# Hybrid encoder: heads in the order B, C, A, two maps scored at once, probabilities turned by half banks, out-projection begun beside the last pair

## The chip, the cores and the metric

The kernel runs on one core of a Trainium2 chip. The metric is the device time of one execution in microseconds (us), as the median of several runs.

## The reference, cut to what matters

Two layers of mixing and MLP over 1024 positions of width 1024, all in float32, then a last RMSNorm. The mixing has 4 differential heads (A, two softmax maps each, values 128 wide), 4 windowed heads with sinks (B, a window of two blocks of 128) and 4 forgetting heads (C, causal, with a cumulative gate).

```python
for l in range(DEPTH):                       # DEPTH = 2
    h = rmsnorm(x, g_mix[l])
    proj = h @ w_in[l]                       # q, k, v of A, B, C and the gates of C
    # A, per head, for each block of 128 queries against all keys up to its end:
    s = q @ k.T * scale - slope * |pos_q - pos_k|         # two maps m = 0, 1
    a = softmax(s[0]) - lam * softmax(s[1])
    o_a = rmsnorm(a @ v, a_subln[l]) * (1 - lam_init)
    # B: the same with one map, a window of 128 keys, and a sink in the softmax's sum
    # C: one map
    s = q @ k.T * scale + cum[q] - cum[k]    # cum = cumsum(log_sigmoid(cf + bias))
    o_c = softmax(where(pos_k <= pos_q, s, NEG)) @ v
    x = x + concat(o_a, o_b, o_c) @ w_out[l]
    h = rmsnorm(x, g_mlp[l])
    x = x + square(relu(h @ w_up[l])) @ w_down[l]         # 1024 -> 4096 -> 1024
return rmsnorm(x, g_final)
```

## The kernel before

Activations lie transposed: feature chunks of 128 on the partitions, 1024 positions along the free dimension. Every large product is done in a split form: an operand becomes a high part (rounded to the matmul's format, a copy on ScalarE) and a low part (the difference, on VectorE), and three products high x high, high x low, low x high are added in PSUM. A **slab** is one 128-column strip of a weight matrix times all positions. It has 8 **pieces** (one per chunk of 128 inputs, `piece`, line 1192, and `products`, 1136), each of 6 matmuls of 512 columns. A weight slab is loaded in two DMAs on SyncE's queue into the single buffer `w_raw` (`load`, 366) and split into one of two slots (ScalarE 477 and 525, VectorE 809 and 841). The next load waits for that split.

The kernel has five instruction streams written out by hand, one per engine, each in its own order, tied by counting semaphores. A wait in a stream holds all that stands behind it.

A layer goes so. The 23 input slabs give gates, then q, k and v for eight **pairs**: an A pair is one head with its two maps, a C pair two heads, a B pair two query heads that share keys. A slab's result is scaled out of PSUM into `part` (`evacuate`, 847), copied to the high part (527) and subtracted to the low part (843); values are turned first by eight transposes (`turn`, 1153). From the fifth slab on, the pieces stand as filling between the steps of attention, for the pair after the current one.

`Run` (105) plans attention: `RUN_A` (two A pairs, executed twice by a loop), then `RUN_C`, then `RUN_CB` (the second C pair and both B pairs). `PIECES` and `END_PIECES` (99, 100) give the pieces beside each step; the last B pair has none, the first 8. An A step is one block of 128 queries with both maps, a C step one head of a block (16 a pair), a B step both heads of a block. `attend` on TensorE (1303) does in step t: scores of t (`scores`, 1259: three matmuls of up to 512 columns for each 512 keys, with only 64 contracted rows, map 0 on partitions 0 to 63, map 1 on 64 to 127), pieces, values of step t-2 (1283), in A the second map's scores, the transposes of step t-1 (`turn_probs`, 1271), pieces. All maps of A and C go through the same PSUM tensor `ps[0]`, one after another; B's two maps take a bank each.

```python
for at in range(0, width, BANK):
    w = min(BANK, width - at)
    for p, (q, k) in enumerate(((q_hi, k_hi), (q_hi, k_lo), (q_lo, k_hi))):
        mm = nc.tensor.matmul(ps[0][:, p0 + at:p0 + at + w], q[half, qs, i * P:(i + 1) * P],
                              k[half, ks, k0 * P + at:k0 * P + at + w], start=(p == 0), stop=(p == 2))
```

VectorE adds the position bias and takes the row maximum of a map in one custom instruction over its whole width (`biased_max`, 933, instruction at 940), scales it (946, 948), combines A's two maps (`combine`, 952 to 961), takes the low half of the turned probabilities (922, at 925 for the first four blocks, 929 for the rest) and sums the value parts (979). ScalarE does the exponentials with their row sums (632), the high half of the turned probabilities (600, 604), the finished outputs (615 to 627), and for C a bias of the key's and the query's cumulative gate (594, with 1003 on VectorE). Its gate rows are spread over the partitions by matmuls (`spread`, 1214): heads 0 and 1 before attention, 2 and 3 between `RUN_C` and `RUN_CB`. In each step ScalarE has: turned probabilities, exponentials, outputs, weight split. A turned step of up to 1024 columns fills `ps[2]`, both banks, so the next one's transposes wait for its low part (`pt_split`).

After the last step the eight head outputs are turned and split (`turn_out`, 1391; 702, 1052), with the first out-projection slab's pieces between them (1408), then the other seven slabs, each added to `xt`. That region held the head outputs during attention, so x was spilled to DRAM in one 4 MB DMA on SyncE's queue ahead of the third slab's load (396) and comes back in two of 2 MB (406). Then the MLP: 64 slabs, `up` and `down`, with ScalarE and VectorE taking the next weights before the hidden values (`split_w` ahead of `hidden`, 731 and 1093).

## Time and profile before

| what | us |
|---|---|
| three runs, median (lowest to highest) | 2849.33 (2838.36 to 2854.39) |
| the profiled execution | 2837.89 |
| its span, first to last instruction | 2835.8 |
| granted clock of TensorE over the span | 0.965 of full |
| TensorE busy | 2723.2 |
| VectorE, ScalarE, GpSimd busy | 1226.4, 958.7, 92.5 |

The profile is of one execution of its own, 2837.89 us, which lies at the low end of the three runs. Busy times are sums over the span. Matmuls overlap in the pipeline, so the mean duration of one (389 ns for 512 columns) is longer than the distance from one to the next. "PE" is TensorE's matmuls, "PEld" its weight loads, "DVE" VectorE, "ACT" ScalarE, "POOL" GpSimd, "SP" SyncE, and L1149 is line 1149 of the kernel. PEclk is the share of full clock that was granted in a fortieth of the span.

### The profile page before, as it was taken

The page shows a single profiled execution, that of the slowest core. Times are in us where ns is not written, and L with a number is a line of the kernel's source. Part 1 is how long each engine was busy: PE and PEld are TensorE (multiplying, and loading weights), DVE is VectorE, ACT ScalarE, POOL GpSimd, SP SyncE. Part 2 cuts the span into 40 slices and gives each one's busy share as a digit, 9 for nine tenths or more (in the row PEclk, how much of TensorE's full clock was granted, in tenths as well). Part 3 has the DMA queues.
Part 4 walks back from the last instruction along what each step waited for, and adds up shares of the span by engine and source line. Part 5 has one row for each costly group of instructions (what it writes and reads, how often), then busy time and mean ns, then how long its engine had stood idle before and what let it go on. Part 6 is the DMA issues. An engine that isn't in the chain of part 4 may idle for free.

```text
span 2835.8 us, 35362 instructions
## 1 busy us (share of the span) xinstructions
PE 2723.2 (96%) x12809; PEld 2211.0 (78%) x12809; DVE 1226.4 (43%) x2444; ACT 958.7 (34%) x1700; POOL 92.5 (3%) x51
## 2 busy tenths in 40 slices
PE   7999999979999999999999999998899999999998
PEld 6777777768888888888877777776788888888887
DVE  5565665654322322223436666656443223232334
ACT  4444454552321212112234444545423122130223
POOL 0000010001000000000200001000020000000001
PEclk9999999959999999999999999998899999999998
DMA  4100000012111111111130000000211111111112
GB/s 153 38 23 23 22 23 16 8 38 82 45 52 45 47 50 49 47 50 46 44 104 23 23 22 23 16 23 8 82 52 45 45 51 48 48 44 52 44 52 74
DMA packets 214389, 126.25 MB, mean 45 GB/s; under 512 B 14702, under 2 KB 213400, under 8 KB 213528
## 3 DMA queue, kind: packets, MB, share of 16 engines
q1 hardware_dynamic: 211176, 121.95, 14.4%
q10 hardware_dynamic: 3120, 3.15, 0.3%
q8 instruction: 48, 0.79, 0.1%
q14 instruction: 45, 0.37, 0.0%
HBM read 112.49 MB, written 12.58 MB: 44 GB/s over the span
## 4 chain that ended last, share of the span: by engine, by line
PE 84%; DVE 6%; ACT 4%; issue 3%; DVEq 1%; DMA 1%; SPq 0%; ACTq 0%; POOL 0%; POOLq 0%
PE ps L1149 54%; PE ps L1196 17%; PE ps L1266 5%; PE ps L1296 2%; PE ps L1278 1%; ACT probs L632 1%; PE ps L1298 1%; DVE probs L940 1%; PE ps L1155 1%; DVEq L943 1%; DVE part L856 1%; PE ps L1408 1%; PE ps L1218 1%; DVE neg_max L948 1%; DVE part L853 1%
## 5 line engine op out<-in xcount | busy, mean ns | idle before, releaser
L1149 PE MATMUL ps<-h_hi,w_hi 128*128 128x512 f32 x1024 | 315.6, 389 | 0.0
L1060 DVE TENSOR_TENSOR xt<-ps,xt 128x1024 f32 (+1 forms) x80 | 98.0, 1225 | 503.1 <-PE ps L1149 501.6
L1149 PE MATMUL ps<-h_lo,w_hi 128*128 128x512 f32 x1024 | 315.3, 389 | 0.0
L1149 PE MATMUL ps<-u_hi,w_hi 128*128 128x512 f32 x1024 | 315.2, 389 | 0.0
L1149 PE MATMUL ps<-u_lo,w_hi 128*128 128x512 f32 x1024 | 315.2, 389 | 0.0
L1149 PE MATMUL ps<-h_hi,w_lo 128*128 128x512 f32 x1024 | 315.2, 389 | 0.0
L1149 PE MATMUL ps<-u_hi,w_lo 128*128 128x512 f32 x1024 | 315.2, 389 | 0.0
L477 ACT ACTIVATE w_hi<-w_raw 128x1024 fp32r<-128x1024 f32 x144 | 151.2, 1050 | 454.8 <-PE ps L1149 436.5
L1196 PE MATMUL ps<-h_hi,w_hi 128*128 128x512 f32 x736 | 265.5, 443 | 34.4 <-DVE v_parts L845 12.7
L1196 PE MATMUL ps<-h_lo,w_hi 128*128 128x512 f32 x736 | 237.4, 405 | 0.0
L1196 PE MATMUL ps<-h_hi,w_lo 128*128 128x512 f32 x736 | 235.0, 401 | 0.0
L720 ACT ACTIVATE ring<-ring 128x1024 f32<-128x1024 f32 x64 | 67.8, 1060 | 487.1 <-DVE ring L1080 487.1
L1149 PEld LDWEIGHTS ps<-h_lo,w_hi 128*128 128x128 f32 x1024 | 192.2, 188 | 40.0
L1149 PEld LDWEIGHTS ps<-h_hi,w_lo 128*128 128x128 f32 x1024 | 192.2, 188 | 40.0
L1149 PEld LDWEIGHTS ps<-u_lo,w_hi 128*128 128x128 f32 x1024 | 192.2, 188 | 39.9
L1149 PEld LDWEIGHTS ps<-u_hi,w_hi 128*128 128x128 f32 x1024 | 192.2, 188 | 39.9
L1149 PEld LDWEIGHTS ps<-u_hi,w_lo 128*128 128x128 f32 x1024 | 192.2, 188 | 39.9
L1149 PEld LDWEIGHTS ps<-h_hi,w_hi 128*128 128x128 f32 x1024 | 191.9, 188 | 39.6
L1080 DVE SCALAR_TENSOR_TENSOR ring<-ps,inv_rms 128x1024 f32<-128x1024 f32 x64 | 78.4, 1225 | 322.9 <-PE ps L1149 311.0
L1296 PE MATMUL ps<-v_parts,pt_hi 128*128 128x128 f32 (+1 forms) x696 | 182.0, 327 | 24.6 <-DVE pt_lo L929 18.6
L632 ACT ACTIVATE probs<-probs,neg_max,slope_now 128x256 f32<-128x256 f32 (+7 forms) x128 | 111.2, 868 | 255.7 <-DVE neg_max L946 255.5
L1196 PEld LDWEIGHTS ps<-h_hi,w_hi 128*128 128x128 f32 x736 | 120.9, 195 | 87.4 <-issue 57.3
(159 smaller groups left out, 4000.3 us busy)
## 6 DMA issues: line engine op xcount, KB each, us to landing
w_raw<-in_w_up_dram SPq DMA_DIRECT2D x128, 256.0 KB, 3.1
w_raw<-in_w_down_dram SPq DMA_DIRECT2D x128, 256.0 KB, 3.0
w_raw<-in_w_in_dram SPq DMA_DIRECT2D x92, 256.0 KB, 3.3
x_saved<-xt SPq DMA_DIRECT2D x2, 4096.0 KB, 11.9
w_raw<-in_w_out_dram SPq DMA_DIRECT2D x32, 256.0 KB, 3.0
xt<-x_saved SPq DMA_DIRECT2D x4, 2048.0 KB, 7.4
out_dram<-rows SPq DMA_DIRECT2D x4, 1024.0 KB, 5.6
rows<-in_x_dram ACTq DMA_DIRECT2D x3, 1024.0 KB, 14.0
```

What stands on the lines that cost most here:

```text
L477: nc.scalar.activation(w_hi[:, j], w_raw[:], ACT.Copy).then_inc(w_hi_done, 1)
L632: e = nc.scalar.activation(probs[:, n % 4, 0:width], probs[:, n % 4, 0:width], ACT.Exp, bias=neg_max[:, n % 8:n % 8 + 1], scale=sl, accum_ ...
L720: nc.scalar.activation(ring[j][:], ring[j][:], ACT.Square)
L853: e = V.scalar_tensor_tensor(out=part[:], in0=ps[p][:], scalar=q_scale[:, bass.ds(pair, 1)], in1=inv_rms[:], op0=ALU.mult, op1=ALU.mult)
L856: e = V.tensor_tensor(part[:], ps[p][:], inv_rms[:], ALU.mult)
L940: V.tensor_tensor_reduce(out=probs[:, n % 4, 0:width], in0=ps[0][:, p0:p0 + width], in1=bias, scale=1.0, scalar=-3e38, op0=ALU.add, op1=AL ...
L1060: V.tensor_tensor(xt[:, 2 * m + j], r, xt[:, 2 * m + j], ALU.add).then_inc(evacuated, 1)
L1080: V.scalar_tensor_tensor(out=ring[j][:], in0=r, scalar=0.0, in1=inv_rms[:], op0=ALU.max, op1=ALU.mult).then_inc(evacuated, 1)
L1149: mm = nc.tensor.matmul(ps[j][:, bass.ts(t, BANK)], w[:, j, c], h[:, c, bass.ts(t, BANK)], start=(c == 0 and n == 0), stop=(c == NC - 1 an ...
L1196: mm = nc.tensor.matmul(ps[p][:, bass.ts(t, BANK)], w[:, j, c], h[:, c, bass.ts(t, BANK)], start=(c == 0 and n == 0), stop=(c == NC - 1 an ...
L1266: mm = nc.tensor.matmul(ps[0][:, p0 + at:p0 + at + w], q[half, qs, i * P:(i + 1) * P], k[half, ks, k0 * P + at:k0 * P + at + w], start=(p ...
L1296: nc.tensor.matmul(o.rearrange("p (h e) -> p h e", h=2), pt_hi[:, b0 + k * blocks + b], v_parts[:, slot, k0 + b, :, e0:e1], start=(b == 0) ...
```

## The change

The order of pairs becomes B, B, C, C, A, A, A, A, planned in one list of **slots**, with no loop or seam between groups. A step is now always a block of 128 queries with both of its maps: 64 steps a layer, where there were 80. Key changes:

- **Scores.** Both maps are scored at once, passes outermost, map 0 into bank 0 and map 1 into bank 1 of `ps[0]`. Maps wider than 512 are done in two phases. C's mask is added by a matmul of the identity with the causal block, and its bias is the key's gate alone; ScalarE's and VectorE's bias instructions go.
- **Half banks.** Turned probabilities go through PSUM by halves of at most four blocks, which alternate over the two banks of `ps[2]`; each slot has at most one half. In a slot TensorE does scores, half of the pieces, the turn of one half, the values of the half before it, the second phase's scores, the other pieces.
- **Pieces.** B pairs have two pieces a step; A and C pairs begin with none, then two to four.
- **Out-projection.** The finished heads are turned in halves beside the last pair (`MIX_AT`), and slabs 0 to 2 run there over six of the eight chunks; their last two chunks follow later from one extra load (`EXTRA`). x comes back chunk by chunk during the last pair.
- **Gates.** All four gate rows are spread before attention.
- **x's spill** is 8 DMAs on ScalarE's queue, one behind each chunk's high part.
- **MLP.** Hidden values come ahead of the next weights' split on ScalarE and VectorE.
- Two regions of SBUF change roles from layer to layer, so that mixed outputs are not written over q, k, v.

```diff
-    PIECES = {"A": [4, 4, 3, 3, 2, 3, 3, 2], "C": [1] * 4 + [2] * 6 + [1, 2, 1, 2, 1, 1], "B": [2] + [1] * 6 + [0]}
-    END_PIECES = {"A": [4, 4, 3, 3, 2, 2, 2, 2, 2], "C": [2] * 7 + [1] * 9 + [1], "B": [0] * 9}
+    ORDER = [("B", 0), ("B", 1), ("C", 0), ("C", 1), ("A", 0), ("A", 1), ("A", 2), ("A", 3)]
+    PIECES = {0: [2] * 8, 1: [2] * 8, 2: [0, 3, 4, 4, 4, 4, 3, 2], 3: [0, 3, 4, 4, 4, 4, 3, 2]}
+    for p in range(FIRST_A, PAIRS - 1):
+        PIECES[p] = [0, 4, 4, 4, 3, 3, 3, 3]
+    PIECES[PAIRS - 1] = [0, 1, 3, 4, 4, 3, 3, 0]
+    MIX_AT = {56: [0, 1], 57: [2, 3], 58: [4, 5], 62: [6]}
...
+    for t in range(NT + 1):
+        mine = []
+        if t:
+            grp, b = ORDER[(t - 1) // NQ][0], window(t - 1)[1]
+            if grp == "A":
+                mine = [add_half(t - 1, [(0, at, min(4, b - at))]) for at in range(0, b, 4)]
+            elif 2 * b <= 4:
+                mine = [add_half(t - 1, [(0, 0, b), (1, 0, b)])]
+            else:
+                mine = [add_half(t - 1, [(j, at, min(4, b - at))]) for j in range(2) for at in range(0, b, 4)]
+            mine[-1].last = True
+        for slab in MIX_AT.get(t, []):
+            mine += [add_half(None, [(0, 4 * side, 4)], slab, side) for side in range(2)]
...
+        if n and slots[n - 1].ends is not None:
+            e = slots[n - 1].ends
+            s.split = [e + 2] if e + 2 < EXTRA else []
+            if e + 2 == EXTRA - 1:
+                s.split.append(EXTRA)
...
+            at = 0 if phases(t) == 1 else 1 + j
+            now[min(at, len(now) - 1)].exps.append(j)
...
-                sp.dma_start(x_saved, xt[:].rearrange("p c s -> p (c s)")).then_inc(x_spilled, 16)
+            def spill(c):
+                act.dma_start(x_saved[:, c], xt[:, c]).then_inc(x_spilled, 16)
+                def restore(c):
+                    sp.wait_ge(turned, NHALF * l + mix_ready[c])
+                    sp.dma_start(xt[:, c], x_saved[:, c]).then_inc(x_back[c], 16)
...
@@ ScalarE, attention @@
+                for s in slots:
+                    if s.half:
+                        half_high(s.half)
+                    if s.ended is not None and s.ended < IN:
+                        part_high(s.ended)
+                    for j in s.exps:
+                        exponentials(s.step, j)
+                    if s.summed is not None:
+                        finish_o(s.summed)
+                    for n in s.split:
+                        split_load(l, n)
...
@@ VectorE, attention @@
+                    if s.first and t:
+                        if ORDER[(t - 1) // NQ][0] == "A":
+                            combine(t - 1)
+                    if s.first and t < NT:
+                        biased_max(t, 0)
+                    if s.half:
+                        half_low(s.half)
+                    if s.first and t < NT and phases(t) == 2:
+                        biased_max(t, 1)
...
@@ TensorE, scores @@
+                    for n, (q, k) in enumerate(((q_hi, k_hi), (q_hi, k_lo), (q_lo, k_hi))):
+                        for j in range(2):
+                            half = slice(j * HD, (j + 1) * HD)
+                            mm = T.matmul(ps[0][:, BANK * j:BANK * j + key1 - key0], q[half, q_slot(p), i * P:(i + 1) * P],
+                                          k[half, kv_slot(p), k0 * P + key0:k0 * P + key1],
+                                          start=(n == 0), stop=(n == 2 and not masked))
...
+                def turn_half(half):
+                    if NHALF * l + half.index > 1:
+                        pe.wait_ge(pt_split, NHALF * l + half.index - 1)
...
+                for s in slots:
+                    t = s.step
+                    early = (len(s.pieces) + 1) // 2
+                    if s.first and t < NT:
+                        scores(t, 0)
+                    dense(s.pieces[:early])
+                    if s.half:
+                        turn_half(s.half)
+                    if s.values:
+                        values(s.values)
+                    if s.turns_v is not None:
+                        pe.wait_ge(evacuated, EVACS * l + slab_of(s.turns_v, V_) + 1)
+                        turn(part, ps[1], NQ, v_turned)
+                    if s.first and t < NT and phases(t) == 2:
+                        scores(t, 1)
+                    dense(s.pieces[early:])
...
-                        split_w(l, 1, NC * g + m + (NC // 2 + j), 1 - j)
-                        hidden(g, m, j)
+                            hidden(g, m, j)
+                            next_weights(16 * g + 2 * m + j, j)
```

## Rows read from the trace of the kernel before

**Rows 1.** The page: span, TensorE, one of six equal groups of the feed-forward part.

```profile
span 2835.8 us, 35362 instructions
...
PE 2723.2 (96%) x12809; PEld 2211.0 (78%) x12809; DVE 1226.4 (43%) x2444; ACT 958.7 (34%) x1700; POOL 92.5 (3%) x51
...
PEclk9999999959999999999999999998899999999998
...
L1149 PE MATMUL ps<-h_hi,w_hi 128*128 128x512 f32 x1024 | 315.6, 389 | 0.0
...
```

**Rows 2.** Stretches of layer 0: length, busy us per engine, granted clock, DMA share, GB/s.

```profile
...
84.40:223.20 138.80, 132.85 (x665) 103.68 (x664) 87.07 (x232) 62.16 (x147) 0.00 (x0) 0.99 0.09 24
223.20:364.00 140.80, 133.05 (x666) 103.76 (x664) 88.76 (x234) 63.00 (x150) 0.00 (x0) 0.99 0.09 23
364.00:450.60 86.60, 82.49 (x443) 65.89 (x441) 51.23 (x146) 46.51 (x98) 7.56 (x4) 0.94 0.08 19
450.60:456.30 5.70, 5.70 (x8) 1.83 (x8) 2.65 (x3) 2.28 (x3) 0.00 (x0) 0.62 0.29 75
456.30:541.10 84.80, 81.30 (x436) 64.66 (x437) 48.38 (x151) 44.06 (x97) 0.00 (x0) 0.94 0.06 14
541.10:618.20 77.10, 61.66 (x330) 50.20 (x328) 44.10 (x187) 44.55 (x139) 0.00 (x0) 0.67 0.03 8
618.20:643.20 25.00, 22.69 (x115) 18.51 (x115) 11.84 (x10) 10.39 (x11) 0.00 (x0) 0.84 0.34 126
...
```

**Rows 3.** The chain of waits, 643 to 800 us: start, us, what.

```profile
...
643.36 87.04 PE ps L1149 x384
...
```

**Rows 4.** The chain of waits in an A pair of layer 1.

```profile
...
1502.28 0.89 PE ps L1266 x3
1503.17 1.58 PE ps L1196 x6
...
```

**Rows 5.** A step of B: TensorE groups with shapes, then the timeline (start, us, ...).

```profile
...
L1266 PE MATMUL ps<-k_hi,q_hi 64*128 64x256 f32 x2 | 0.4, 383 | 0.4 <-DVE row_max L940 0.4
...
557.99 0.39 PE L1266 MATMUL ps<-k_hi,q_hi 64*128 64x256 f32 x2 [0.39 <-DVE row_max L940]
...
558.55 0.73 PE L1196 MATMUL ps<-h_hi,w_hi 128*128 128x512 f32 x2
...
```

**Rows 6.** TensorE in the timeline of an A pair: eight transposes.

```profile
...
218.59 1.09 PE L1278 MATMUL ps<-ident,probs 128*128 128x128 f32 x8
...
```

**Rows 7.** TensorE in the timeline of B: values, with a dense piece between and without.

```profile
...
556.52 0.33 PE L1296 MATMUL ps<-v_parts,pt_hi 128*128 128x128 f32 x1 [0.31 <-DVE pt_lo L929]
...
556.76 0.30 PE L1296 MATMUL ps<-v_parts,pt_hi 128*128 128x128 f32 x1
...
556.99 0.31 PE L1296 MATMUL ps<-v_parts,pt_hi 128*128 128x128 f32 x1
...
569.89 0.48 PE L1296 MATMUL ps<-v_parts,pt_hi 128*128 128x128 f32 x1 [0.50 <-DVE pt_lo L929]
...
```

**Rows 8.** Groups of VectorE and of ScalarE by shape: xcount, busy us, mean ns, idle before.

```profile
...
L841 DVE TENSOR_TENSOR w_lo<-w_raw,w_hi 128x1024 fp32r<-128x1024 f32 x44 | 53.9, 1225 | 60.8 <-ACT w_hi L525 60.8
L925 DVE TENSOR_TENSOR pt_lo<-ps,pt_hi 128x512 fp32r<-128x512 f32 x64 | 44.1, 688 | 47.5 <-ACT pt_hi L600 46.9
...
L940 DVE CUSTOM_DVE_ANT_0 probs<-ps,far 128x512 f32<-128x512 f32 x16 | 11.0, 689 | 2.0 <-issue 2.0
L961 DVE SCALAR_TENSOR_TENSOR probs<-probs,lam_ratio 128x1024 f32<-128x1024 f32 x8 | 10.3, 1286 | 0.6
...
L600 ACT ACTIVATE pt_hi<-ps 128x512 fp32r<-128x512 f32 x64 | 37.2, 582 | 0.0
...
L530 ACT ACTIVATE q_hi<-part 128x1024 fp32r<-128x1024 f32 x16 | 16.7, 1043 | 6.7 <-DVE part L853 6.7
...
L632 ACT ACTIVATE probs<-probs,neg_max,slope_now 128x1024 f32<-128x1024 f32 x16 | 19.9, 1242 | 33.6 <-DVE neg_max L946 33.6
...
```

**Rows 9.** The chain of waits, 30 to 60 us.

```profile
...
38.21 12.76 DMA w_raw<-in_w_in_dram
...
```

More of the change, by code:

```diff
@@ new lines, in hybrid_encoder @@
+    last = None
+    for n, s in enumerate(slots):
+        s.values = last.half if last and last.half and last.half.slab is None else None
+        if s.values and s.values.last:
+            s.summed = s.values.step
+        done = slots[n - 1].ends if n else None
+        if done is not None and (done >= IN or SLABS[done][1] != V_):
+            s.ended = done
+        if s.turns_v is not None:
+            assert s.ended is None
+            s.ended = slab_of(s.turns_v, V_)
+        if n and slots[n - 1].ends is not None:
[3 more added lines that the diff above has]
+                s.split.append(EXTRA)
+        last = s
```

1577 lines of the change are left out of this document (781 added, 796 removed).

## The prediction, made before the change was run

> **What bounds the kernel now.** I read the page first. TensorE is busy 96% of the span, VectorE 43% and ScalarE 34% [rows 1], so the question is what TensorE's own sequence holds that could go. The profiled execution took 2837.9 us (span 2835.8); the three timed runs have their median 11 us higher, 0.4%, which is about what a measurement of this kernel can tell from no change (0.5%). I work against 2837.9.
>
> Second, the table of stretches for layer 0 [rows 2]. 84.4 to 364 are the four A pairs, two in each of two passes through one loop body: 139.8 us a pass, 69.9 a pair. 364 to 450.6 is the first C pair, 450.6 to 456.3 a seam in which only gate rows are spread, 456.3 to 541.1 the second C pair, 541.1 to 618.2 both B pairs, 618.2 to 643.2 the turning of the eight heads' outputs with the first out-projection slab among it, and 643.2 to 719.6 the other seven slabs. The last, 7 slabs of 48 matmuls, is 76.2 by the price below. Together 635 us. The reader should see that the clock column says 0.99 in A and 0.94 in C, but 0.67 in B and 0.84 in the turning: TensorE runs there for a good part at the lower of its levels, 1.2 GHz, having waited often just before.
>
> Third, the chain of waits gives prices. 384 dense matmuls of 512 columns take 87.04 us [rows 3], so a piece of 6 costs 1.36. The feed-forward part is nothing but such pieces and stays as it is: six groups of 1024 such matmuls, one of which stands in [rows 1], at 0.227 us are 1393 us of the 2838, and the change can't touch them. Beside attention a piece that TensorE has just switched to shows 1.58, and the three passes of one map's 512 columns 0.89 against 3 x 0.227 = 0.68 [rows 4]. So a switch costs about 0.2 us each way.
>
> **What scoring two maps at once is worth.** Before, only B issues its two maps one behind the other. There two matmuls of mean 383 ns stand in 0.4 us together, and what TensorE does next, a dense piece, begins 0.56 us after the first of all six [rows 5]. Six of 256 columns end to end would be 6 x 0.107 = 0.64 plus the switch. Map 0 (partitions 0 to 63) and map 1 (64 to 127) thus already run beside each other. The Trainium skill (TensorE: Matmul & The Clock Gate, LDWEIGHTS step and "Packing small matmuls") says that matmuls keep program order, and only weight loads are pulled ahead. By that, B, which issues three passes of map 0 and then three of map 1, would gain from the new interleaving too, 0.3 us on each of 32 steps, 10 us; the row contradicts it, and my sum gives B nothing.
>
> **The A pair, part by part** (sum before first, so that the terms can be trusted). 24 pieces 32.6; two maps of 36 blocks, 27648 columns at 0.443 ns, 12.2, in 16 segments at 0.21, 3.4; 36 transposes at 0.11 (eight take 1.09 with the last one's latency [rows 6]) 4.0; 36 blocks of values at 0.23 (starts 0.23 apart [rows 7]) 8.3; turning V 1.1. That is 61.6 of the measured 69.9; 28 switches to dense pieces at 0.22 (6.2) and the loop's seam (2) make up the rest. After: columns halve to 6.1, but maps over 512 wide come in two phases, so there are 12 segments, 2.5; the rest stays, with 24 switches, 5.3: 59.9 us if nothing else waits. That is the lower end.
>
> Something does wait, for the changed order shortens the distance between links. A step's chain is: VectorE combines the two maps, TensorE turns a half bank, ScalarE copies it, VectorE takes the low part, the second phase is reduced, and both exponentials run, behind the second half's copy on ScalarE. Widest step, from the end of one combine: first phase's two reductions, 0.69 each with handovers, to 1.55; half low to 2.3; second phase's scores have landed by 2.9, its two reductions and the maximum end at 5.1; TensorE, with two and then one piece between, turns the second half by 6.2, its copy ends at 6.75; two exponentials, 1.24 each and the read of their sums, end at 9.4; combine, 1.29 behind two small operations, 1.9: 11.4 us. TensorE has 7.9 of work in it, so it stands 3.5. In the sixth step (768 wide) a K slab ends: evacuation 1.22, ScalarE's part copy 1.04 ahead of the exponentials, and after them the next weights' split, 1.05 and 1.23, ahead of the combine in both queues: 13.5 against 8.8, 4.7 lost. The other steps lose about 3 together. All latencies in series give 71; that is the upper end. I take 67: nearer to it, since every duration is a row [rows 8], less some slack that narrow steps hand on. VectorE needs some 50 us a pair, so it isn't the bound by volume. Three pairs: 201.
>
> **The last A pair** has 18 pieces, not 24 (-8.2), and 14 half banks of mixed output: turns 14 x 0.44, and 0.4 each for the bank to come free, 12. One weight load (the last two chunks' rows for three slabs) is asked for only after the split before it, so ScalarE stands for a split, an issue and a landing, 3 to 5 us, in front of exponentials. 74.
>
> **The C pair.** Before 85.7 on average. After: pieces 32.6, scores 6.1 + 2.5, 32 mask matmuls of 128 columns 0.9 when paired, transposes 72 x 0.11 = 7.9, values 72 x 0.225 = 16.2, V 1.1, some 30 switches 6.6: 74. The bias leaves ScalarE and VectorE (the query's cumulative gate drops out of a softmax), which cost nothing before, as both hid behind TensorE. 22 half banks replace 16 turns; where a slot has no piece, copy 0.58 + low 0.69 + handovers 0.25 stand against 0.9 + 0.44 of values and turn: 3 us. 77; the ends are 74 and 85.7. Two pairs 154, and the seam of 5.7 goes.
>
> **The B pair** now has 16 pieces: 21.8, scores 8 x 0.56 = 4.5, transposes 3.3, values 6.8, V 0.6, switches 3.5, waits 1.5: 42. Two pairs 84 with 32 pieces in them, at the full clock, where 77.1 held 8 at 0.67. ScalarE's 44.6 us in the old stretch are 2.8 a step, against a new step of 5.2, so it doesn't bind.
>
> **Around them.** Out-projection: 64 pieces, 18 in the last pair, 46 left, 62.6, plus the last turns and values 4 and a 2 us wait for the last two halves: 69. Two more spreads and their four copies on ScalarE stand ahead of attention: 2. New: 2 + 84 + 154 + 201 + 74 + 69 = 584 against 635.2; 51 a layer, 102 in all.
>
> At the start a weight load lies 12.76 us behind the 4 MB spill of x on SP's queue [rows 9]. The spill moves to ScalarE's queue, in 8 parts from the first chunk on, so SP's load is issued 10 us sooner. ScalarE issues 8 transfers among its copies, and this part waits on it: -7; the ends are 0 and -10. The Trainium skill (DMA: Bandwidth & Descriptors, "Issuing engines are not separate DMA queues") says that both queues run on the same 16 engines and interleave. By that the bytes still contend, and the sum would be 7 us higher. The restore of x becomes eight transfers of 512 KB beside the last pair; it is needed only when its slab ends. In the feed-forward part ScalarE now takes the hidden copies ahead of the next weights: steady slabs have 10.9 us for some 6, but the third slab of each layer waits on the spread of the root, the copy 1.0, ring 1.2, two copies 2.1, split 2.3: 2 us late, +4 in all.
>
> Sum: 2837.9 - 102 - 7 + 4 = 2733; with half of the profiled run's distance to the median, 2735.
>
> **The rivals.** (1) TensorE stays the only bound: slack covers every chain, A at 60, C at 74. 7 x 8 + 3 x 4 = 68 less: 2667. For it: VectorE at 63% and ScalarE at 45% of the A stretches. Against: the worked chains. (2) Slower: each half bank exposes its round trip. ScalarE and VectorE take 0.59 + 0.69 + 0.25, and only the previous half's values, 0.9, cover it: 0.6 for 124 halves a layer (48 in A, 44 in C, 16 in B, 16 mixed), 149 in all: 2884. It decides from 0.42 a half on, where the 105 us are gone. For it: TensorE stands 0.31 before values with a piece between and 0.50 without one [rows 7]. Against: 170 pieces lie between 124 halves. (3) The pairing doesn't hold at 512 columns in two banks: 6.1 us on 12 pairs, +73: 2808. Against it rows 5. (4) The chains bind fully and C gains nothing for its half banks: A at 71, C at 84: 16 a layer for A's, 14 for C's: about 2793.
>
> **How the numbers follow.** Forecast (2700 to 2770) 0.48; rival 1 0.22; rival 4 0.15; rival 3 0.05; rival 2 0.10, of which some 0.06 ends over 0.5% slower and 0.03 near nothing. The range reaches from just below rival 1 to just above rival 4: 2660 to 2800. Faster by over 0.5%: 0.90; within: 0.04; slower: 0.06.
>
> **What would show it.** Score matmuls of 512 columns in pairs some 10 ns apart, all through A and C; the clock at 0.99 or more from the first B pair to the end of the layer; B pairs of 42, C of 77, A of 67 us; TensorE's waits in A ahead of transposes, for the combine, in the steps of 768 and 1024; no long wait for a weight load at 38 us. I am wrong if waits for the low parts outweigh those for the combine (rival 2), if A pairs fall near 60 (rival 1), or if paired scores start 0.2 us apart (rival 3).

## The result, and the profile after

The changed kernel takes 2892.4 us in the median of 4 runs (2886.7 to 2896.2), the kernel before 2846.4 beside it: ratio 1.016, 95% interval 1.0125 to 1.0195. It is 1.6% slower where I forecast 3.7% faster, and outside the range. The profiled execution took 2891.7 us against 2837.9.

The page of the changed kernel, to be held against [rows 1]:

```profile
span 2889.9 us, 34048 instructions
...
PE 2678.5 (93%) x12857; PEld 2177.3 (75%) x12857; DVE 1195.1 (41%) x2409; ACT 897.7 (31%) x1580; POOL 88.6 (3%) x49
...
PEclk9998899988999999999999989998899999999998
```

TensorE is busy 45 us less than before and the span is 54 us longer, so some 99 us of standing were added. The clock row of layer 0 no longer has one deep slice, but four shallow ones of 0.8, two over the end of C and the start of A and two over the last A pair and the out-projection. The stretches of layer 0 answer to [rows 2]; the columns are length, busy us of TensorE, its weight loads, VectorE, ScalarE and GpSimd, granted clock, DMA share, GB/s:

```profile
84.40:123.20 38.80, 37.84 (x215) 29.68 (x216) 21.06 (x86) 23.35 (x69) 0.00 (x0) 0.94 0.09 25
123.20:164.00 40.80, 38.48 (x237) 30.32 (x236) 26.40 (x98) 25.99 (x77) 0.00 (x0) 1.00 0.10 27
164.00:246.90 82.90, 73.47 (x423) 58.98 (x422) 40.68 (x118) 33.88 (x77) 0.00 (x0) 0.93 0.07 20
246.90:339.70 92.80, 83.24 (x457) 68.64 (x456) 41.91 (x120) 34.29 (x77) 0.00 (x0) 0.87 0.07 18
339.70:421.50 81.80, 71.97 (x359) 57.06 (x358) 42.97 (x125) 26.24 (x64) 0.00 (x0) 0.84 0.08 20
421.50:496.50 75.00, 62.72 (x333) 48.71 (x332) 44.41 (x126) 27.97 (x67) 0.00 (x0) 0.93 0.08 22
496.50:575.10 78.60, 64.51 (x334) 49.97 (x332) 46.42 (x129) 30.83 (x70) 3.75 (x2) 0.89 0.07 21
575.10:743.30 168.20, 138.48 (x669) 111.91 (x668) 93.48 (x175) 65.22 (x115) 18.21 (x8) 0.88 0.18 53
```

The lines are B, B, C, C, three A pairs, and the last A pair with the out-projection. B is 79.6 where I had 84. C is 175.7 for 154, A 235.4 for 201, the rest 168.2 for 143. That is 659 for 582, 77 us too long: 22 in C, 34 in the three A pairs, 25 in the last stretch, and 4 gained in B. In layer 1 it is some 8 less, as its C pairs and first three A pairs take 403 us for 411. The second A pair is the plain case: 62.7 us of work at a clock of 0.93 in 75.0 us.

What TensorE waits for, whole kernel (total us, times, longest), from the waits by line:

```profile
PE ps L1263 <- DVE probs L920: 84.1, 41, 6.0
PE ps L1115 <- DVE part L800: 32.1, 12, 3.3
PE ps L1283 <- DVE pt_lo L943: 22.4, 22, 2.8
```

The first is a transpose waiting for A's combination, the second a dense piece waiting for the evacuation of the slab before it, the third the values waiting for the low part of a half bank. To see why, I followed one case in the second A pair, at the step of 768 keys. TensorE in the timeline (start, us, engine, line, operation, tiles, shapes, count, idle before and who ended it):

```profile
465.96 0.28 PE L1210 MATMUL ps<-k_hi,q_lo 64*128 64x256 f32 x2
469.22 0.70 PE L1115 MATMUL ps<-wide_hi,w_hi 128*128 128x512 f32 x2 [2.98 <-DVE part L800]
...
478.10 0.66 PE L1263 MATMUL ps<-ident,probs 128*128 128x128 f32 x2 [2.34 <-DVE probs L920]
```

VectorE in the same timeline:

```profile
466.29 0.42 DVE L888 CUSTOM_DVE_ANT_0 probs<-ps,far 128x256 f32<-128x256 f32 x1
...
467.16 0.46 DVE L904 TENSOR_SCALAR neg_max<-row_max,far_max,neg_slope 128x1 f32<-128x1 f32 x2
...
467.86 1.21 DVE L800 TENSOR_TENSOR part<-ps,inv_rms 128x1024 f32<-128x1024 f32 x1
...
475.21 1.23 DVE L765 TENSOR_TENSOR w_lo<-w_raw,w_hi 128x1024 fp32r<-128x1024 f32 x1 [1.75 <-ACT w_hi L516]
...
476.94 1.02 DVE L920 SCALAR_TENSOR_TENSOR probs<-probs,lam_ratio 128x768 f32<-128x768 f32 x1
```

And ScalarE:

```profile
470.99 0.28 ACT L627 ACTIVATE pt_hi<-ps 128x128 fp32r<-128x128 f32 x1 [2.61 <-PE ps L1263]
471.16 1.05 ACT L572 ACTIVATE k_hi<-part 128x1024 fp32r<-128x1024 f32 x1
472.11 1.02 ACT L609 ACTIVATE probs<-probs,neg_max,slope 128x768 f32<-128x768 f32 x1
```

The slab had ended by 463.4. VectorE holds its evacuation until 467.86, behind the second key phase's maximum, whose scores TensorE issues only after its turn; the next piece stands 2.98 us for it. The step's maxima are ready at 467.6, but the exponentials begin at 472.1: ScalarE has put the next half bank's copy first, which needs a turn that TensorE reaches at 470.7, after the pieces it was held up in, and behind that copy K's of 1.05 us. Then VectorE puts the weights' low part (475.21) ahead of the combination. Each queue is in order, and each holds something that waits on another.

### The profile page after: what moved, and what is told of

The parts are those of the page before. It is cut to its first block, busy times and chain, and to the rows that moved or that the text cites. A ratio compares the mean times of both kernels' runs of the same rounds, so it can differ in the third digit from the quotient of the medians.

```text
span 2889.9 us, 34048 instructions
## 1 busy us (share of the span) xinstructions
PE 2678.5 (93%) x12857; PEld 2177.3 (75%) x12857; DVE 1195.1 (41%) x2409; ACT 897.7 (31%) x1580; POOL 88.6 (3%) x49
## 3 DMA queue, kind: packets, MB, share of 16 engines
q1 hardware_dynamic: 213192, 114.35, 13.8%
## 4 chain that ended last, share of the span: by engine, by line
PE 83%; DVE 7%; ACT 5%; issue 3%; DVEq 0%; DMA 0%; SPq 0%; POOL 0%; ACTq 0%; POOLq 0%
PE ps L1115 71%; PE ps L1263 3%; PE ps L1210 3%; ACT probs L609 2%; PE ps L1283 2%; PE ps L1285 1%; DVE probs L920 1%; PE ps L1096 1%; ACT pt_hi L627 1%; DVE w_lo L765 1%; DVE part L800 1%; ACT w_hi L516 1%; PE ps L1160 1%; DVE part L797 1%; DVE wide_lo L938 0%
## 5 line engine op out<-in xcount | busy, mean ns | idle before, releaser
L1115 PE MATMUL ps<-wide_hi,w_hi 128*128 128x512 f32 x3016 | 976.2, 405 | 66.0 <-DVE part L800 32.1
L1115 PE MATMUL ps<-wide_lo,w_hi 128*128 128x512 f32 x3016 | 947.7, 396 | 0.0
L1115 PE MATMUL ps<-wide_hi,w_lo 128*128 128x512 f32 x3016 | 943.8, 394 | 0.0
L1115 PEld LDWEIGHTS ps<-wide_hi,w_hi 128*128 128x128 f32 x3016 | 555.5, 192 | 205.3 <-issue 90.9
L1115 PEld LDWEIGHTS ps<-wide_lo,w_hi 128*128 128x128 f32 x3016 | 578.4, 192 | 125.5
L1115 PEld LDWEIGHTS ps<-wide_hi,w_lo 128*128 128x128 f32 x3016 | 576.1, 191 | 124.3
L1283 PE MATMUL ps<-v_parts,pt_hi 128*128 128x128 f32 (+1 forms) x696 | 203.4, 351 | 22.6 <-DVE pt_lo L943 22.4
L609 ACT ACTIVATE probs<-probs,neg_max,slope 128x256 f32<-128x256 f32 (+7 forms) x256 | 201.3, 788 | 26.2 <-DVE neg_max L900 13.7
L1285 PE MATMUL ps<-v_parts,pt_lo 128*128 128x64 f32 (+1 forms) x696 | 170.7, 253 | 0.0
L1285 PEld LDWEIGHTS ps<-v_parts,pt_lo 128*128 128x128 f32 x696 | 150.1, 216 | 0.1
L765 DVE TENSOR_TENSOR w_lo<-w_raw,w_hi 128x1024 fp32r<-128x1024 f32 x78 | 105.1, 1348 | 94.5 <-ACT w_hi L516 94.5
L1046 DVE TENSOR_TENSOR w_lo<-w_raw,w_hi 128x1024 fp32r<-128x1024 f32 x112 | 136.4, 1218 | 0.5 <-ACT w_hi L683 0.5
## 6 DMA issues: line engine op xcount, KB each, us to landing
first_rows<-in_x_dram ACTq DMA_DIRECT2D x3, 1024.0 KB, 13.4
```

Source lines behind the costliest of these rows:

```text
L609: e = A.activation(probs[:, (2 * t + j) % 4, 0:width], probs[:, (2 * t + j) % 4, 0:width], ACT.Exp, bias=neg_max[:, at:at + 1], scale=sl, ...
L765: V.tensor_tensor(w_lo[:, j], w_raw[:], w_hi[:, j].bitcast(F32), ALU.subtract).then_inc(w_split, 1)
L1046: V.tensor_tensor(w_lo[:, z], w_raw[:], w_hi[:, z].bitcast(F32), ALU.subtract).then_inc(w_split, 1)
L1115: mm = T.matmul(ps[p][:, bass.ts(t, BANK)], w, h[:, bass.ts(t, BANK)], start=(start and n == 0), stop=(stop and n == 2))
L1283: T.matmul(o.rearrange("p (h e) -> p h e", h=2), pt_hi[:, bank, at], v_parts[:, kv_slot(p), k0 + b, :, e], start=(b == 0), stop=False)
L1285: mm = T.matmul(o[:, 0:w], pt_lo[:, bank, at], v_parts[:, kv_slot(p), k0 + b, 0, e], start=False, stop=(b == blocks - 1))
```

## The experiments

Theory Q (queues): the new written order puts late work ahead of urgent work in the queues of VectorE and ScalarE and leaves wide steps without pieces, and the clock takes a second toll behind the waits. Theory H is my second rival: every half bank's round trip is exposed. Theory W: TensorE's own work or clock, whatever the queues do. All ratios are to the kernel before, beside which each was timed.

| run | median us | ratio | 95% interval |
|---|---|---|---|
| the change | 2892.4 | 1.0160 | 1.0125 to 1.0195 |
| exponentials first | 2884.9 | 1.0157 | 1.0130 to 1.0184 |
| earlier evacuation | 2855.9 | 1.0054 | 1.0031 to 1.0078 |
| no combination | 2798.1 | 0.9845 | 0.9821 to 0.9870 |
| both, and later weight split | 2875.7 | 1.0121 | 1.0094 to 1.0148 |
| filler in the waits | 2875.8 | 1.0119 | 1.0098 to 1.0139 |
| evacuation, V first | 2833.1 | 0.9969 | 0.9957 to 0.9981 |
| and exponentials first in two steps | 2820.9 | 0.9933 | 0.9910 to 0.9955 |
| evacuation, pieces moved | 2808.2 | 0.9887 | 0.9864 to 0.9910 |
| scores map after map | 2886.7 | 1.0158 | 1.0132 to 1.0183 |
| no low part | 2859.8 | 1.0053 | 1.0030 to 1.0077 |
| these four together | 2796.8 | 0.9828 | 0.9811 to 0.9845 |
| and mixed output first | 2794.6 | 0.9818 | 0.9798 to 0.9838 |
| the change, extra split later | 2872.6 | 1.0088 | 1.0063 to 1.0113 |
| the change, scaling sooner | 2886.2 | 1.0138 | 1.0111 to 1.0165 |
| all that gained | 2771.6 | 0.9755 | 0.9724 to 0.9785 |
| and last pair's pieces moved | 2783.6 | 0.9777 | 0.9753 to 0.9801 |

**Exponentials first.**

```diff
+if not s.first:
+    for j in s.exps: exponentials(s.step, j)
 if s.half: half_high(s.half)
 if s.ended is not None and s.ended < IN: part_high(s.ended)
-for j in s.exps: exponentials(s.step, j)
+if s.first:
+    for j in s.exps: exponentials(s.step, j)
```

> Edit: in a step's second slot ScalarE does the step's exponentials before it copies the half bank (pt_hi) and before part_high; nothing is left out. Theory Q (queues): in the A pairs TensorE waits at the transposes for the combination (84 us in 41 waits of the whole changed kernel), because the exponentials of a two-phase step stand behind pt_hi, and so behind TensorE's next turn, although their maxima are ready 2 to 4 us before. Then this edit gives 30 us, 20 to 50, off the changed kernel's 2892: ratio to the kernel before 0.999 to 1.009. Theory H (half banks): the round trips of the half banks are what costs; pt_hi now stands behind 2 us of exponentials, so this run is slower than the changed kernel by 10 to 30 us. Theory W (TensorE's own work and clock, whatever the queues): no change, within 5 us.

Measured 1.0157: nothing gained. Q expected too much, and H's part isn't empty. The waits of the whole run:

```profile
PE ps L1267 <- DVE probs L924: 76.0, 37, 6.0
PE ps L1287 <- DVE pt_lo L947: 26.5, 22, 2.7
```

8 us of waits for the combination went and 4 came back ahead of values. A step's length here runs from its first scores to those of the next step. In the trace the seventh step of the second A pair fell from 13.4 to 8.3 us, while the sixth rose from 12.3 to 13.9 and the last C steps from 12 to 15. An order that suits one step harms another.

**Earlier evacuation.**

```diff
 if s.half: half_low(s.half)
+soon = s.ends is not None and s.ends < IN and len(s.pieces) == 1 and s.first
+if soon: evacuate(s.ends)
 if s.first and t < NT and phases(t) == 2: biased_max(t, 1)
```

> Edit: where a slab ends in the early piece of a step's first slot, VectorE evacuates it before the second key half's maximum instead of after it; nothing is left out. Theory Q: the pieces that wait about 3 us for an evacuation (12 waits, 32 us over the kernel) wait because evacuate stands behind that maximum, which waits for scores that TensorE issues after its turn. Some half of them are of this form: 8 us off 2892, 3 to 18. Theory H and theory W: no change, within 4 us.

1.0054: 1.1% back by moving one instruction in seven places a layer, some 30 us where 8 were expected and 18 was the upper end.

```profile
PE ps L1268 <- DVE probs L920: 83.2, 40, 5.9
PE ps L1120 <- DVE part L800: 11.3, 11, 1.2
```

The waits for the evacuation fell by 20.8 us, those for the combination by 0.9, and the time by some 30. The part above 22 has no wait of its own; the clock is the candidate. Of the two C pairs the first bears it out, and in the second it stays where it was:

```profile
164.30:241.20 76.90, 69.64 (x424) 56.25 (x423) 40.28 (x117) 33.24 (x76) 0.00 (x0) 0.98 0.08 21
241.20:330.20 89.00, 82.10 (x459) 67.57 (x458) 42.02 (x120) 34.88 (x78) 0.00 (x0) 0.87 0.07 19
```

The first C pair now takes 76.9 at a clock of 0.98, where the change has 82.9 at 0.93. That it is the 77 I had reckoned is in part luck: it turns B's narrow maps at its start and leaves its own widest to the next pair (424 matmuls for 459), and with the same order of work in C it took 76.3 in the run V first and 80.1 in the run after that.

**No combination.**

```diff
-if ORDER[(t - 1) // NQ][0] == "A": combine(t - 1)
-pe.wait_ge(combined, NQ * AH * l + half.step - NQ * FIRST_A + 1)
+pe.wait_ge(exp_done, 2 * NT * l + 2 * half.step + 1)
```

> Edit: the combination of the two maps in the A pairs is left out (the first map's probabilities are turned as soon as their own exponential is done), so that output is not the reference's; everything else stays. Theory Q: nearly all of the 84 us of waits for the combination go, and part of the clock lost behind them: 60 us off 2892, 40 to 90, and the granted clock of the second A pair of layer 0, 0.93 now, rises to 0.97 or more. Theory H: VectorE is freed of 1 to 1.4 us per step, 10 to 20 us off. Theory W: within 10 us, clock as before.

0.9845: some 90 us off, near the upper end of Q. The second and third A pair:

```profile
411.90:475.30 63.40, 57.37 (x336) 45.22 (x334) 34.86 (x102) 27.97 (x67) 0.00 (x0) 1.00 0.10 26
475.30:539.90 64.60, 58.72 (x335) 46.32 (x334) 35.38 (x105) 30.68 (x70) 3.75 (x2) 0.97 0.09 25
```

63.4 us at 1.00 for 75.0 at 0.93, with the same matmuls: TensorE's busy time falls by 5.4 us because they run faster. H's 10 to 20 us are out.

**Exponentials first, earlier evacuation, and `split_load` a slot later** (outside the last pair `slots[n + 2].split` takes what `slots[n + 1].split` took).

> Edit: the exponentials first, the evacuation before the second maximum, and the split of the next weights one slot later on both engines (outside the last pair); nothing is left out. Theory Q: the queues' delays before the exponentials and before the combination go together: 45 us off 2892, 25 to 80, that is level with the kernel before or better. Theory H: slower than the changed kernel by 10 to 30 us, as for the exponentials alone. Theory W: within 8 us of it.

1.0121, slower than the earlier evacuation alone (1.0054): a miss for Q's number. The traces show where: the sixth step of the A pairs takes 15.0 to 16.3 us, where the earlier evacuation alone has 10.6, 10.6 and 14.5. In the second A pair the split's low part, moved a slot later, now stands ahead of the combination of 640 keys on VectorE, and TensorE waits 3.16 us for that combination instead of 0.79:

```profile
453.18 1.23 DVE L771 TENSOR_TENSOR w_lo<-w_raw,w_hi 128x1024 fp32r<-128x1024 f32 x1 [2.90 <-ACT w_hi L518]
...
454.90 0.88 DVE L926 SCALAR_TENSOR_TENSOR probs<-probs,lam_ratio 128x640 f32<-128x640 f32 x1
```

The later split wasn't run by itself, so its share of the loss isn't known.

**Filler in the waits.**

```diff
+FILLER = {0: 28, 6: 16, 7: 8}
 dense(s.pieces[:early])
+if s.first and FIRST_A * NQ < t < 7 * NQ and t % NQ in FILLER:
+    pe.wait_ge(o_summed, NT * l + t - 2)
+    for _ in range(FILLER.get(t % NQ, 0)):
+        T.matmul(ps[3][:, BANK * ((t - 1) % 2) + 2 * P:BANK * ((t - 1) % 2) + BANK], ident_r[:],
+                 h_hi[:, 0, 0:2 * P], start=True, stop=True)
 if s.half: turn_half(s.half)
```

> Edit, on the changed kernel: matmuls of 256 columns that no one reads go into a free part of the values' bank, ahead of the transposes that wait for the combination: 28 at the first step of the second and third A pair, 16 in the seventh and 8 in the eighth step of the first three A pairs; nothing is left out. They are meant to fit into the waits of 3.7, 2.3 and 1.2 us that stand there now. Theory C (the waits cost a second time, because TensorE's clock falls to 1.2 GHz behind them): although TensorE has more to do, these pairs get shorter, 4 to 6 us each of their 75 to 79, 25 us off 2892 in all (10 to 40), and their granted clock rises from 0.84 to 0.93 to above 0.95. Rival F (a wait costs what it lasts and the clock falls for another reason): no gain; the same within 4 us, or up to 15 us slower where the filler outlasts a wait.

256 matmuls more, and 1.0119, 0.4% less than the change (the intervals overlap). The trace is clearer. The first line is the filled seventh step of the second A pair, the second that pair, the third the next one:

```profile
469.40:479.40 10.00, 9.86 (x65) 8.17 (x64) 6.69 (x19) 2.94 (x8) 0.00 (x0) 1.00 0.20 54
...
417.08:489.29 72.21, 65.97 (x386) 52.70 (x385) 44.39 (x126) 28.04 (x67) 0.00 (x0) 0.98 0.09 23
489.29:565.40 76.11, 67.80 (x388) 54.00 (x386) 46.41 (x129) 30.86 (x70) 3.75 (x2) 0.96 0.08 22
```

The same step of the change:

```profile
473.19:486.55 13.36, 11.02 (x47) 8.40 (x46) 6.95 (x20) 3.74 (x9) 0.00 (x0) 0.74 0.14 39
```

The step has 16 more matmuls and takes 10.0 us at 1.00 instead of 13.4 at 0.74. The pair takes 2.8 us less, not 4 to 6: the sixth step grew by 1.6. So a wait can be paid twice, once as it lasts and once as TensorE runs at 1.2 GHz in the work that follows. That is theory C, with a smaller number than I gave it.

The second payment isn't fixed by the wait. In the run with scores map after map (below) the same step of layer 1 stands behind waits of 0.76 and 2.99 and has one of 2.34 in it, as in the change, and yet:

```profile
1884.60:1895.42 10.82, 8.15 (x47) 6.13 (x46) 6.97 (x20) 3.76 (x9) 0.00 (x0) 1.00 0.19 50
```

For one and the same order of waits the step takes 10.8 to 13.4 us, at 1.00 to 0.74. I counted the seventh steps of the first three A pairs in both layers. In the six traces that keep a wait of 0.9 us or more in it (the change, map after map, no low part, the extra split later, scaling sooner, earlier evacuation) 26 of 36 are at 0.74 to 0.86 and 10 at 1.00. With the wait filled, or nearly gone as with the exponentials first, all 12 are at 1.00. What tips the clock in one execution and not in the other stays open.

**V first** (on the earlier evacuation; in TensorE's slot loop), **exponentials first in two steps** (on that; the cut shows its condition against that of exponentials first), and **pieces moved** (on the earlier evacuation):

```diff
+if s.turns_v is not None: pe.wait_ge(...); turn(part, ps[1], NQ, v_turned)
 dense(s.pieces[:early])
 if s.half: turn_half(s.half)
 if s.values: values(s.values)
-if s.turns_v is not None: pe.wait_ge(...); turn(part, ps[1], NQ, v_turned)
...
-if not s.first:
+if not s.first and s.step >= FIRST_A * NQ and s.step % NQ in (5, 6):
     for j in s.exps: exponentials(s.step, j)
...
-PIECES = {..., 2: [0, 3, 4, 4, 4, 4, 3, 2], 3: [0, 3, 4, 4, 4, 4, 3, 2]}
+PIECES = {..., 2: [0, 2, 3, 4, 4, 4, 4, 3], 3: [0, 2, 3, 4, 4, 4, 4, 3]}
-    PIECES[p] = [0, 4, 4, 4, 3, 3, 3, 3]
+    PIECES[p] = [0, 3, 3, 3, 3, 4, 4, 4]
```

> Edit, on the kernel with the earlier evacuation (2856): at a pair's first step the turn of the values' slab goes ahead of the transposes that wait 3.7 us for the combination, instead of behind them. Theory Q: 1.1 us of work goes into each of the waits of 10 seams, and V's split ends sooner: 10 us off 2856, 5 to 18. Rival (the seam is bound by the chain of max, exponentials and combination itself): the same within 4 us, since the step ends no sooner.

> Edit, on the previous run: in the sixth and seventh step of the A pairs alone the exponentials go before the half bank's copy. The run with this in all steps took 5 us from the seventh step (13.4 to 7.9) and gave 1.6 to 2.7 us back in the sixth steps and in the last step of the C pairs, where pt_hi came late. Theory Q: 20 us off the previous run, 8 to 35. Theory H (a copy of a half bank made late always costs what the exponentials gain): the same within 5 us.

> Edit, on the kernel with the earlier evacuation (2856): the dense pieces per step go from 0,4,4,4,3,3,3,3 to 0,3,3,3,3,4,4,4 in the A pairs and from 0,3,4,4,4,4,3,2 to 0,2,3,4,4,4,4,3 in the C pairs; the sum stays. Theory Q: cover moves from steps of 128 to 512 keys, where TensorE waits little, to those of 768 to 1024 keys, where it waits 1.2 to 2.3 us: 15 us off 2856, 5 to 30. Rival (the short steps live on their pieces, and their own chain comes out): the same within 5 us or up to 15 us slower.

V first: 0.9969 from 1.0054, about 24 us, above its range. The two steps: 0.9933, 10 us more (the intervals part, just), in Q's range though below its 20. Moving pieces: 0.9887 from 1.0054, 47 us, half as much again as the upper end. Its second A pair:

```profile
390.42:456.96 66.54, 59.70 (x333) 46.22 (x332) 44.27 (x125) 27.93 (x67) 0.00 (x0) 0.97 0.09 25
```

This is the 67 us I had forecast, with no piece added or removed; the first and the third take 70.3 and 71.4.

**Scores map after map.**

```diff
-for n, (q, k) in enumerate(((q_hi, k_hi), (q_hi, k_lo), (q_lo, k_hi))):
-    for j in range(2):
+for j in range(2):
+    for n, (q, k) in enumerate(((q_hi, k_hi), (q_hi, k_lo), (q_lo, k_hi))):
```

> Edit, on the changed kernel: the score matmuls are issued map after map (three passes of map 0, then three of map 1) instead of pass after pass; nothing is left out. If the two maps' row halves run beside each other whatever the order inside the group, as the B rows of the kernel before suggested: the same time as the changed kernel's 2892 within 5 us, and scores still about 0.9 us per 512-column phase of two maps. If matmuls keep program order (the page's rule): 0.7 us more per full phase, 12 pairs of A and C, some 70 us more less what falls into waits: 30 to 70 us slower.

1.0158, the change's own time. The pairs stand in its timeline as in the change's, two and two within 10 ns, though each is issued three matmuls after its partner. Two matmuls of 512 columns, 493 ns each, take 0.50 us together (the first line is the timeline, the others give duration in ns least, median and most, and first and last start):

```profile
443.81 0.50 PE L1210 MATMUL ps<-k_hi,q_hi 64*128 64x512 f32 x2
...
L1210 PE MATMUL ps<-k_hi,q_hi x2: 493/493/493, 443.8 to 443.8; 64*128 64x512 f32 x2
L1210 PE MATMUL ps<-k_hi,q_lo x2: 386/390/393, 444.4 to 444.4; 64*128 64x512 f32 x2
```

So the pairing, here in two row halves and two banks, doesn't need the interleaving; one bank for both wasn't tried. Rival 3 is out.

**No low part.** `half_low` subtracts one column instead of all, and in `values`:

```diff
-mm = T.matmul(o[:, 0:w], pt_lo[:, bank, at], v_parts[:, kv_slot(p), k0 + b, 0, e],
+mm = T.matmul(o[:, 0:w], pt_hi[:, bank, at], v_parts[:, kv_slot(p), k0 + b, 0, e],
```

> Edit, on the changed kernel: the low part of the turned probabilities is left out (VectorE writes one column of it and TensorE multiplies the high part twice), so the output is not the reference's; TensorE's work stays, and each half bank's round trip is some 0.5 us shorter on VectorE. Theory Q: the waits for low parts (22 us in 22) go, and VectorE reaches maxima and combinations a little sooner: 25 us off 2892, 10 to 45. Theory H (my second rival: 0.6 us exposed on every one of some 250 half banks): 75 us or more off.

1.0053: 30 us, where my second rival priced 149 us for all half banks. Values still wait, for shorter times (15.2 us in 23 waits, for 22.4 in 22). The second C pair gains most, 7.7 us: its waits for low parts fall from 4.5 to 2.0 us and its clock rises from 0.87 to 0.92:

```profile
243.40:328.50 85.10, 78.24 (x459) 64.08 (x458) 32.44 (x119) 34.13 (x77) 0.00 (x0) 0.92 0.07 19
```

**Together** (earlier evacuation, V first, the two steps, pieces moved), and **mixed output first** (`mine` at step 56 begins with one head's two half banks, ahead of the A halves). Their edits are those above and:

```diff
+if t == 7 * NQ: mine = [add_half(None, [(0, 4 * side, 4)], MIX_AT[t][0], side) for side in range(2)]
```

> Edit: the earlier evacuation, V's turn ahead of the first step's transposes, the exponentials first in the sixth and seventh step of A, and the pieces moved to the wide steps, together; nothing is left out. If what each gave adds up (e9's 2808, less 20 and less 10): 2780, between 2765 and 2800, ratio to the kernel before 0.974 to 0.986. If they all bought the same waits: 2800 to 2810.

> Edit, on the previous run: at the last pair's first step, 16 to 18 us long, the two half banks of one head of mixed output are turned before the transposes that wait for the combination, instead of behind them. Theory Q: they fill 1 to 2 us of the wait: 4 us off the previous run over two layers, 1 to 8 (which this measurement can hardly tell), and that step 1.5 us or more shorter in the trace. Rival (that step is bound by the half banks' own round trips with no piece between): the step stays as long.

0.9828 and 0.9818. The parts don't add up wholly: together they are 17 us beyond the moved pieces, where V first and the two steps had given 24 and 10 on the earlier evacuation. Mixed output first makes its step 13.6 us instead of 15.0 in the trace, but no difference that the median can tell.

**The last pair.** Left over were 25 us a layer in the last A pair and the out-projection.

```diff
-if e + 2 == EXTRA - 1: s.split.append(EXTRA)
+if s.ends is not None and s.ends + 2 == EXTRA - 1: slots[n + 3].split.append(EXTRA)
```

> Edit, on the changed kernel: in the last A pair the split of the extra weight load (the last two chunks' rows of three slabs) is done two slots later on ScalarE and VectorE, so that no exponentials stand behind a transfer that has only just been asked for; nothing is left out. If that load is a good part of what the last pair takes beyond its reckoning (TensorE waits 5.9 us for a combination at 648.8): 8 us off 2892 over two layers, 3 to 15, and that wait of 5.9 falls below 3. If another link (evacuation, VectorE's order) ends last there: the same within 3 us, the wait as long.

1.0088, some 20 us off, above its range. ScalarE in the change's timeline:

```profile
643.95 0.84 ACT L510 ACTIVATE xw_hi<-w_raw 128x768 fp32r<-128x768 f32 x1 [4.37 <-DMA w_raw<-in_w_out_dram]
...
644.85 1.01 ACT L609 ACTIVATE probs<-probs,neg_max,slope 128x768 f32<-128x768 f32 x1
```

It stands 4.37 us for a transfer asked for only after the split just before, with the exponentials behind it; TensorE then waits 5.85 us at its transposes. In the run with the split later that wait is 0.76 us, and the seventh step, of 896 keys, is 10.8 us long instead of 18.2. What is left of the stretch's waits there:

```profile
PE ps L1264 <- DVE probs L921: 14.0, 7, 4.3
PE ps L1264 <- DVE wide_lo L939: 4.4, 4, 1.6
```

Scaling sooner, on the change:

```diff
-SCALE_AT = {FIRST_A * NQ + 2 * NQ + 3: (0, 2), FIRST_A * NQ + 3 * NQ + 3: (2, 3)}
+SCALE_AT = {FIRST_A * NQ + 2 * NQ + 2: (0, 2), FIRST_A * NQ + 3 * NQ + 2: (2, 3)}
```

> Edit, on the changed kernel: the scaling of finished heads on GpSimd begins one step sooner in the third and fourth A pair; nothing is left out. In the trace one combination of 640 columns takes 2.42 us where its like take 0.9, exactly while GpSimd scales. If the two hold each other up when they run at once: the slow combination moves to the neighbouring step (512 columns) or goes, and the waits of the fifth turn with it; 3 us off at most, not to be told in the median, but plain in the trace. If the 2.4 us had another cause, the 640-column one stays slow.

1.0138, not to be told from the change, as expected. What its trace shows of GpSimd stands in the last section.

Then all of it together, and on that the last pair's pieces:

```diff
-PIECES[PAIRS - 1] = [0, 1, 3, 4, 4, 3, 3, 0]
+PIECES[PAIRS - 1] = [0, 1, 2, 3, 3, 3, 3, 3]
```

> Edit: everything that gave something, together: the kernel with mixed output first (2794.6) plus the extra load's split two slots later and the scaling one step sooner. If the last pair is bound as the two previous theories say: 2785, between 2775 and 2792. If not: 2790 to 2798.

> Edit, on the previous run: the 18 out-projection pieces of the last A pair go from 0,1,3,4,4,3,3,0 to 0,1,2,3,3,3,3,3, so that its widest step, which has none, gets three. If the distance between score and turn is what the last pair lacks (waits of 3.7 and 4.1 us in its last two steps): 8 us off the previous run over two layers, 3 to 15. If the last pair is bound by the half banks of mixed output at its start and end: the same within 3 us.

All that gained, together: 2771.6 us, ratio 0.9755, 2.4% faster than the kernel before, and below what was expected of it. Its third A pair, and its last pair with the out-projection:

```profile
449.20:513.80 64.60, 58.65 (x335) 44.60 (x334) 45.62 (x128) 30.56 (x70) 4.20 (x2) 1.00 0.09 25
513.80:673.00 159.20, 134.66 (x669) 108.39 (x669) 92.31 (x175) 63.22 (x113) 18.25 (x8) 0.91 0.19 56
```

Pieces in the last pair's widest steps bought nothing (0.9777, intervals overlapping): in the trace the pair's first seven steps take 75.3 us for 74.2, with 13.1 for 11.6 in the sixth. Whether the half banks of mixed output bind there stays open. So do some 16 us a layer between 159 and the 143 reckoned.

## Why the prediction was wrong, point by point

**The bound and the price list** held. A piece, a transpose, a block of values cost what the rows said, B came out at 79.6 for 84, and TensorE's busy time did fall.

**Two maps at once** held, at 512 columns too. The step that the Trainium skill spoke against (TensorE: Matmul & The Clock Gate, "The mechanism": matmuls start and end in the order of the program) is settled by the run map after map, with 2 x 493 ns in 0.50 us and 1.0158 for 1.0160: the measurement decides.

**The step that failed is the one from 71 to 67 in the A pair, "less some slack that narrow steps hand on", and beside it a clock that the sum takes as full.** The second A pair of layer 0 shows each term. Its work, 59.9 in the sum, is 57.4 at full clock in the run without combination. I had worked 3.5 of standing for the widest chain, 4.7 for the sixth step and "about 3" for the others, 11.2 in all, and let only 7 of it count; TensorE stood 12.3. The clock had no term and cost 5.4, as 62.7 of busy time against 57.4. 57.4 + 12.3 + 5.4 make 75.1, for the 75.0 measured. No slack was handed on.

The places of the standing I had only in part. The widest chain was sound: it takes 10.4 us from combination to combination where I had 11.4, and TensorE stands for it at the next pair's first step, which has no piece.

```profile
425.71 0.63 PE L1263 MATMUL ps<-ident,probs 128*128 128x128 f32 x4 [3.67 <-DVE probs L920]
```

The sixth step's 13.5 agrees by luck with the 12.3 and 13.8 measured in the first two pairs (the third has 15.6). 3 us of it are a dense piece that stands for an evacuation, and the step takes 10.6 in both once that is moved. I named the evacuation as 1.22 us on the chain, and never asked what stands ahead of it on VectorE. The late combination that I had worked for that step falls into the seventh, as a wait of 2.3: of its 13.4 us some 8 are work, 2.3 the wait and 3 the clock. The other four waits make 3.2. The runs give each change a price: 30 us for the evacuation, 24 for V first, 47 for moved pieces, 90 for all waits on the combination, the clock's part included.

**"The clock at 0.99 or more from the first B pair"** was the second failure. [rows 2] had shown 0.67 in B and 0.84 in the turning, where waits were many, and I read it as a cost the change would remove, not as the price of any new wait. The change spreads waits of up to 6 us over the 580 us a layer from the first C pair on, and gets 0.84 to 0.93. In one pair the filler gave back 2.8 us net, and the run without combination 5.4 us of busy time.

**C at 77** failed for the same two reasons, evacuations and clock. With the evacuation moved, the first C pair is 76.9; the second stays at 89, because after a C pair's widest step the next pair's first step has no piece, and that step takes 13.5 us. The waits for low parts were as I had them, 7.1 us in 9 waits in the two pairs, for 3 a pair.

**The last pair and the out-projection, 74 + 69,** took 168.2. I saw the weight load in front of the exponentials and priced the stand at 3 to 5 us; ScalarE did stand 4.37, but the widest steps follow, TensorE waited 5.85, and 10 us a layer went once it was moved. The term of 3 to 5 was mis-sized by at least half; some 15 of the stretch's 25 us too many lie elsewhere.

**The start, -7,** came out at 0: attention begins at 84.4 us in both. The 7 us of waiting for a weight load are gone, so the spill's move did what it should; but two more spreads stand there, and TensorE's eight spread matmuls take 4.35 us, after waits of 1.32 and before one of 1.11, where I had 2. **The feed-forward part, +4,** came out at some 8, 4.1 a layer: the stretch from the last out-projection sum to the layer's last is 705.3 us for 701.2, with one wait of 2.2 us at the third slab.

**The rivals.** Rival 2 had the sign and nearly the time, 2884, and the wrong mechanism: low parts cost 30 us, not 149. Its chance of 0.06 for slower was too small because I let the one slower case carry a single price. The 71 that I called "all latencies in series" was no upper end: a bound made of the latencies on one path leaves out what each queue has ahead of them.

## What to carry to other kernels

When an order is written out by hand and the links of a chain move closer, list for every step what stands ahead of each link in its own queue and what that waits for; look first at the step after the widest, above all where it has no filling (here the longest wait of the plain A pair, 3.67 us). Give every new wait of TensorE a second term for the clock, read from stretches with waits like it, and give it as a range (here 0 to 2.6 us for the same waits). Move one instruction and measure before giving up a restructuring: a handful of such moves took this one from 1.6% slower to 2.4% faster.

## What the runs showed of the hardware

VectorE's combination is held up while GpSimd scales. In the change one combination of 640 columns takes 2.42 us, where its like take 0.89; with the scaling a step sooner it is the one of 512 columns that takes 2.07, and the 640 one is no longer slow. GpSimd in the changed kernel's timeline, then VectorE:

```profile
536.52 3.75 POOL L498 TENSOR_TENSOR o_out<-o_out,o_inv 128x1024 f32<-128x1024 f32 x2 [533.29 <-DVE o_inv L974]
...
538.53 2.42 DVE L920 SCALAR_TENSOR_TENSOR probs<-probs,lam_ratio 128x640 f32<-128x640 f32 x1
```

And with the scaling sooner:

```profile
529.48 4.20 POOL L498 TENSOR_TENSOR o_out<-o_out,o_inv 128x1024 f32<-128x1024 f32 x2 [526.25 <-DVE o_inv L974]
...
529.86 2.07 DVE L920 SCALAR_TENSOR_TENSOR probs<-probs,lam_ratio 128x512 f32<-128x512 f32 x1
```

GpSimd's pair ends at 540.27 in the first case, and the combination 0.68 us later, as if it had begun its data only then. In the second GpSimd's pair takes 4.20 us for 3.75, so it is held up as well. The Trainium skill (SBUF — State Buffer, "Who interferes with whom") says that a VectorE instruction with two inputs in SBUF contends with a GpSimd instruction that reads SBUF, for a port pair that one of them locks; the trace agrees. In the third A pair TensorE then waits 2.3 us, where the pair before has 0.8. By the Trainium skill's same section a VectorE instruction with one SBUF input would not have contended, which no run here tried.

The other finding is that the clock can fall in stretches with waits of only 1 to 3 us: the seventh step ran at 0.74 after a wait of 2.98 and with one of 2.34 in it, and at 1.00 with the second one filled; but with both waits standing it also ran at 1.00 in another trace.
